# A hybrid decoder layer on one core: the first window group's keys projected transposed, three groups of transfers issued from other places

## The reference

```
u = rmsnorm(x, g_pre) @ w_in                          # (tokens, 10256)
for g, (win, dil) in enumerate(((128, 1), (512, 4), (2048, 16))):
    q, k, v = dq[:, :, g], dk[:, :, g], dv[:, :, g]   # 4 heads of 128
    # prompt: query t reads keys t - dil*m, m = 0..128; the last win rows of (k, v) are an output
    # samples: 8 new queries read keys of a cache of win rows and the new keys
    o_g = softmax(q k^T / sqrt(128)) v ; lse_g
o_b = sum over g of softmax_g(lse) * o_g
m = sigmoid(ga) * (z_a @ w_gla_branch) + sigmoid(gb) * (z_b @ w_dil_branch)
h = x + rmsnorm(m @ w_out, g_post)
y = h + (pe @ w_ple_proj) * sigmoid(h @ w_ple_gate)
```

## Time and profile before

| what | value |
|---|---|
| median of three runs | 2817.8 us (2817.68 to 2823.16) |
| profiled execution, its own time | 2818.61 us |
| its span | 2816.8 us |
| PE busy | 2778.1 us (99%) |
| DVE / ACT / POOL busy | 1080.3 / 871.9 / 386.1 us |
| transfers | 558.36 MB, mean 198 GB/s |

### The profile page before, as it was taken

How to read it: one execution, slowest core, us unless ns; L and a number is a source line. 1 busy time by engine, 2 the same in 40 slices (tenths; PEclk the granted TensorE clock), 3 DMA queues, 4 the chain that set the end, 5 groups by cost and what they waited for, 6 DMA issues and landing times.

```text
span 2816.8 us, 40869 instructions
## 1 busy us (share of the span) xinstructions
PE 2778.1 (99%) x16168; PEld 1458.2 (52%) x16168; DVE 1080.3 (38%) x2401; ACT 871.9 (31%) x1788; POOL 386.1 (14%) x633
## 2 busy tenths in 40 slices
PE   8999999999999999999999989999999899999998
PEld 4444456555545665666555545555544344444444
DVE  6311134444333443344223323333323455555452
ACT  5211034444312222333123321111113444444341
POOL 2000010111311002120011113232200000000000
PEclk9999999999999999999999999999999999999999
DMA  9543454655677566584576759787736966556642
GB/s 282 132 169 130 149 202 151 215 189 202 202 250 275 178 193 205 188 276 157 179 266 219 242 174 326 238 261 244 235 136 199 308 170 174 142 159 178 163 113 57
DMA packets 320399, 558.36 MB, mean 198 GB/s; under 512 B 179114, under 2 KB 184305, under 8 KB 316242
## 3 DMA queue, kind: packets, MB, share of 16 engines
q1 hardware_dynamic: 269154, 296.86, 35.1%
q0 software_dynamic: 51056, 258.89, 27.5%
HBM read 378.96 MB, written 236.79 MB: 219 GB/s over the span
## 4 chain that ended last, share of the span: by engine, by line
PE 95%; DMA 2%; SPq 2%; DVE 1%; issue 0%; POOL 0%; ACT 0%; POOLq 0%; DVEq 0%
PE out L2614 42%; PE out L2183 22%; PE out L2611 15%; PE out L1120 2%; PE out L1105 2%; PE out L2617 2%; PE out L1111 1%; PE out L614 1%; PE out L625 1%; PE out L624 1%; PE out L1403 1%; PE out L1096 1%; PE out L1363 1%; DMA U<-stage 1%; SPq L355 1%; DMA sw_kc<-in_cache_kv_w 0%
## 5 line engine op out<-in xcount | busy, mean ns | idle before, releaser
L2614 PE MATMUL out<-w_hi,xn_hi 128*128 128x512 f16 x1920 | 729.0, 380 | 1.3 <-DVE w_lo L2483 0.7
L2614 PE MATMUL out<-w_lo,xn_hi 128*128 128x512 f16 x1920 | 728.3, 379 | 0.0
L2614 PE MATMUL out<-w_hi,xn_lo 128*128 128x512 f16 x1920 | 728.2, 379 | 0.0
L2514 ACT ACTIVATE stage<-out 128x512 f32<-128x512 f32 (+1 forms) x170 | 99.3, 584 | 900.0 <-PE out L2614 605.4
L2552 DVE TENSOR_SCALAR stage<-out 128x512 f32<-128x512 f32 (+1 forms) x170 | 114.8, 676 | 646.9 <-PE out L2614 424.1
L2614 PEld LDWEIGHTS out<-w_hi,xn_lo 128*128 128x128 f16 x1920 | 188.0, 98 | 227.0 <-issue 0.8
L2614 PEld LDWEIGHTS out<-w_hi,xn_hi 128*128 128x128 f16 x1920 | 188.4, 98 | 207.7 <-issue 6.5
L2614 PEld LDWEIGHTS out<-w_lo,xn_hi 128*128 128x128 f16 x1920 | 188.1, 98 | 200.8 <-issue 0.5
L2611 PE MATMUL out<-xn_hi,w_hi 128*128 128x512 f16 x640 | 242.8, 379 | 0.0
L2611 PE MATMUL out<-xn_hi,w_lo 128*128 128x512 f16 x640 | 242.6, 379 | 0.0
L2611 PE MATMUL out<-xn_lo,w_hi 128*128 128x512 f16 x640 | 242.6, 379 | 0.0
(11 more groups left out here) (318 smaller groups left out, 4007.5 us busy)
## 6 DMA issues: line engine op xcount, KB each, us to landing
out<-in_cache_kv_w POOLq DMA_DIRECT2D x64, 1020.0 KB, 9.6
U<-stage SPq DMA_DIRECT2D x240, 256.0 KB, 4.7
raw<-in_w_in SPq DMA_DIRECT2D x78, 512.0 KB, 5.0
sw_kc<-in_cache_kv_w POOLq DMA_DIRECT2D x24, 1024.0 KB, 12.0
sw_vc<-in_cache_kv_w POOLq DMA_DIRECT2D x24, 1024.0 KB, 9.9
UT<-stage SPq DMA_DIRECT2D x80, 256.0 KB, 3.7
sw_rows<-U POOLq DMA_DIRECT2D x32, 512.0 KB, 7.2
out<-in_cache_kv_w POOLq DMA_DIRECT2D x16, 1008.0 KB, 7.6
```

The costliest lines, as they stand in the source:

```text
L2514: move_out(act, m, lambda o, x: act.activation(o, x, ACT.Copy, scale=1.0 / W_SCALE))
L2614: last = pe.matmul(out[m % 3][:, :], x[:, k, at:at + P], y[:, k, :], start=first, stop=final)
```

## The change

- `U_DK`, the keys of group 0, joins `TURNED`: the 16 prompt tiles of this column come out with features in rows and go to `UT`. For group 0 `load` takes a head's keys from there with one transfer, and the score matmul reads them directly. PE transposes only the last block of each head (four in all), ACT copies it to `kT`, and POOL stores these 128 tokens x 4 heads to the output at step 67 of group 0; ACT waits for that store (`kept_stored`) before it uses `kT` in group 1. POOL's copy of these rows from `U` goes. `load` waits for the scores of the head before last ahead of the keys' load, for all groups.
- The buffers of windows and samples are placed in another order, so that the samples' first loads touch only the buffers of even heads. POOL issues them at slot 515 instead of 522, after `head_done` for head 2 of group 2 and `cutter.done`; the mask's load comes at slot 527, after `windows.done`. DVE begins the samples' buffers after `windows.read`, without waiting for the stores.
- `turn_m(0)` stands in slot 674 right behind `turn_z(1)`, ahead of `turn_pe(1)` and `load_early(2)`, instead of in slot 675.
- `queue_weights` is issued by ACT instead of SP, in the same last slot, also after the projection's last matmul.

```
-TURNED = [U_GQ, U_GK] + [U_DQ + g * WIDTH for g in range(GROUPS)]
+TURNED = [U_GQ, U_GK] + [U_DQ + g * WIDTH for g in range(GROUPS)] + [U_DK]
+T_DK = T_DQ + GROUPS * WIDTH
...
 class Windows:
+    def turns(self, n):
+
+        return n // BLOCKS if n < self.STEPS else HEADS + n - self.STEPS
...
     def load(self, q, g, h):
         s, n = h % 2, g * HEADS + h
-        wait(q, self.turned, (n - 1) * BLOCKS)
-        at = U_DK + g * WIDTH + h * HD
-        for src, dst in self.pieces(self.U[0:SEQ, at:at + HD], self.k[s][:, :, :], g):
-            q.dma_start(dst, src).then_inc(self.k_loaded[s], 16)
+        wait(q, self.turned, self.turns(max((n - 1) * BLOCKS, 0)))
         wait(q, self.scored, (n - 1) * BLOCKS)
+        if g == 0:
+            at = T_DK + h * HD
+            q.dma_start(self.k[s][:, :, :], self.UT[at:at + HD, :].rearrange("p (b i) -> p b i", i=P)).then_inc(self.k_loaded[s], 16)
+        else:
...
+        if g == 0 and r == self.STEPS + 3:
+            q.wait_ge(self.turned_kept, HEADS)
+            q.dma_start(self.kv_prompt[0, 0, :, 0], self.kT[:, :HEADS, :]).then_inc(self.kept_stored, 16)
...
+    def head_done(self, eng, g, h):
+
+        eng.wait_ge(self.summed, (g * HEADS + h + 1) * BLOCKS)
+        eng.wait_ge(self.stored[h % 2], self.moved(g, h))
...
-            wait(pe, self.turned_kept, n)
-            pe.transpose(self.TURN[:, 0:P], self.k[h % 2][:, b, :], self.identity[:, :]).then_inc(self.turned, 1)
+            if g > 0 or b == BLOCKS - 1:
+                wait(pe, self.turned_kept, self.turns(n))
+                pe.transpose(self.TURN[:, 0:P], self.k[h % 2][:, b, :], self.identity[:, :]).then_inc(self.turned, 1)
...
-            pe.wait_ge(self.turned_kept, n + 1)
+            if g > 0:
+                pe.wait_ge(self.turned_kept, self.turns(n + 1))
...
+            kT = self.kT if g > 0 else self.k[h % 2]
...
     def scalar(self, act, g, r):
+            if n == self.STEPS:
+                act.wait_ge(self.kept_stored, 16)
...
+            elif b == BLOCKS - 1:
+                act.wait_ge(self.turned, self.turns(n + 1))
+                act.activation(self.kT[:, h, :], self.TURN[:, 0:P], ACT.Copy).then_inc(self.turned_kept, 1)
...
 class Samples:
     def queue(self, q, r):
-        if r == -5:
+        if r == -12:
             self.load_q(q, 0)
             for p in range(last + 1):
                 self.load_k(q, 0, p)
                 if p == 0:
-                    for x in range(self.RING):
+                    for x in range(3):
                         self.load_rows(q, x)
+        if r == 0:
             q.dma_start(self.mask[:, :], self.mask_in).then_inc(self.mask_loaded, 16)
...
 class Mix:
         if slot == self.MERGE_SLOT + 1:
             self.turn_z(sp, 1)
+            self.turn_m(sp, 0)
             self.turn_pe(sp, 1)
             self.load_early(sp, 2)
...
         if slot == self.MERGE_SLOT + 2:
-            self.turn_m(sp, 0)
...
-            if slot == SAMPLE_SLOT - 5:
+            if slot == SAMPLE_SLOT - 12:
+                windows.head_done(q, GROUPS - 1, HEADS - 2)
+                cutter.done(q)
+            if slot == SAMPLE_SLOT:
                 windows.done(q)
-                cutter.done(q)
...
         def _(sp):
-                if m == COLUMN_TILES * TOKEN_TILES - 1 and half == 1:
-                    for i in range(2):
-                        sp.wait_ge(out_ready[i], COLUMN_TILES * TOKEN_TILES // 2)
-                    mix.queue_weights(sp)
...
         def _(act):
+                    if half == 1 and m == COLUMN_TILES * TOKEN_TILES - 1:
+                        for i in range(2):
+                            act.wait_ge(out_ready[i], COLUMN_TILES * TOKEN_TILES // 2)
+                        mix.queue_weights(act)
```

More of the change, by code:

```diff
@@ L1013, in __init__ @@
         self.result_kept = one("result_kept")
+        self.kept_stored = one("kept_stored")
+    def turns(self, n):
+        return n // BLOCKS if n < self.STEPS else HEADS + n - self.STEPS
     def moves(self, g):
@@ L1075, in left, with read @@
         n = GROUPS * self.STEPS
-        return [(signal, n) for signal in (self.turned, self.turned_kept, self.scored, self.masked, self.top_ready, self.weighed,
+        return [(self.turned, self.turns(n)), (self.turned_kept, self.turns(n))] + [(signal, n) for signal in (self.scored, self.masked, self.top_ready, self.weighed,
                                            self.prob_turned, self.prob_kept, self.summed, self.result_kept)]
+    def head_done(self, eng, g, h):
+        eng.wait_ge(self.summed, (g * HEADS + h + 1) * BLOCKS)
+        eng.wait_ge(self.stored[h % 2], self.moved(g, h))
+    def read(self, eng):
+        eng.wait_ge(self.summed, GROUPS * self.STEPS)
+        eng.wait_ge(self.result_kept, GROUPS * self.STEPS)
     def done(self, eng):
-        wait(eng, self.summed, GROUPS * self.STEPS)
-        for h in range(HEADS - 2, HEADS):
-            wait(eng, self.stored[h % 2], self.moved(GROUPS - 1, h))
+        self.head_done(eng, GROUPS - 1, HEADS - 2)
+        self.head_done(eng, GROUPS - 1, HEADS - 1)
     def at(self, g, i):
@@ L1126, in scalar @@
             n, h, b, _, dil = self.at(g, r)
-            act.wait_ge(self.turned, n + 1)
-            wait(act, self.scored, n - 1)
-            if dil > 1:
+            if n == self.STEPS:
+                act.wait_ge(self.kept_stored, 16)
+            if g > 0:
+                act.wait_ge(self.turned, self.turns(n + 1))
+                wait(act, self.scored, n - 1)
                 if b == 0:
@@ L1192, in __init__ @@
         self.q_places = [(tile, QUAD) for tile in (self.new_k, self.new_v, sb("sw_q", [P, WIDTH]))]
+        self.rows = [sb(f"sw_rows{s}", [P, self.PAIR, WIDTH]) for s in range(self.RING)]
+        self.vc = sb("sw_vc", [P, N_CACHE, WIDTH])
         self.qT = sb("sw_qT", [P, GROUPS * HEADS, QUAD])
         self.kT = [sb(f"sw_kT{s}", [P, HEADS, P]) for s in range(2)]
-        self.rows = [sb(f"sw_rows{s}", [P, self.PAIR, WIDTH]) for s in range(self.RING)]
         self.sT = [sb(f"sw_sT{i}", [P, P]) for i in range(len(ROWED))]
@@ L2263, in run_layer @@
             with ExitStack() as part:
[L2264 removed]
+                windows = Windows((core.bind(part)[0], sem), side, U, UT, a["window_mask"], identity, OG, kv_prompt[0])
         stores = Stores(sem)
@@ L2467, in _ @@
                 mix.pool(pool, t)
-            pool.wait_ge(copied, SHIFTS + 4 * GROUPS * 16)
+            pool.wait_ge(copied, SHIFTS + (4 * GROUPS - 1) * 16)
         def cut_hi_piece(act, i):
@@ L2581, in _ @@
                 if q == SAMPLE_SLOT - 2:
-                    windows.done(dve)
+                    windows.read(dve)
                     samples.start(dve)
```

23 lines of the change are left out of this document (12 added, 11 removed).

## The result

The changed kernel takes 2803.8 us (median of 5 runs, 2802.1 to 2805.0), the kernel before on the same chip 2818.5 (5 runs, 2817.7 to 2823.2): the ratio is 0.9946, interval [0.9935, 0.9958]. It is faster by 14.6 us, where I had forecast 24. The profiled execution took 2802.4 us (before 2818.6), with a span of 2800.5 (before 2816.8).

A forecast was written before the change was run, and what follows sets the result against it. PE, 99% busy, was taken as the bound: its instructions plus three waits. Savings of 6.4 + 10.1 + 7.1 = 23.6 us took the profiled 2818.6 to 2795.0, the median to 2794 us; range 2788 to 2802.

The forecast's parts named there:

- Part 1: Group 0's keys projected transposed: 60 of 64 transpositions on PE go, 0.107 us each, saving 6.4 us.
- rival C: Group 1: ACT's wait for the kept keys' store holds up PE and makes the kernel slower; chance 0.02.
- rival D: Group 0: the keys' transpositions were free, so their removal gives 0 and the time is 2800.6 us; chance 0.05.
- Part 2: Samples' first loads issued earlier by POOL: PE's 8.1 us wait and 2.0 us of half speed go, 10.1 us.
- Part 3: After the last slot: weights on ACT and m of tile 0 turned earlier start branches(2) sooner, saving 7.1 us.
- rival B: After the last slot: weights starve tile 2's loads, PE starts as before, gain there 0, time 2801.3 us; chance 0.11.

The follow-up runs named there:

- m_only: Changed kernel with the weights issued by SP again, m of tile 0 still turned ahead of tile 2's loads; 2800.5 us, ratio 0.9935.
- w_only: Changed kernel with m of tile 0 turned in slot 675 again, behind tile 2's loads, weights still on ACT; 2801.6 us, ratio 0.9939.
- rows_8k: Changed kernel with each weight transfer on ACT cut in two of 1 MB, rows of 8 KB instead of 16 KB; 2802.6 us, one run.
- ahead: Changed kernel with tile 2's loads and the transpositions of z(1) and pe(1) issued by SP two slots sooner; 2799.8 us, ratio 0.9932.
- ahead_z: Kernel of ahead with z(2)'s transposition also put before SP's wait for the last tile's store; 2791.2 us, ratio 0.9900.
- p1_only: Changed kernel with only the transposed keys of group 0 kept; samples' loads, m and weights issued as before; 2809.7 us, ratio 0.9967.
- p3_undone: Changed kernel with m of tile 0 turned in slot 675 and the weights issued by SP again; 2800.2 us, ratio 0.9934.
- early_first: Changed kernel with tile 2's five loads issued ahead of the three turns on SP; 2800.1 us, ratio 0.9931.
- rows_2k: Changed kernel with each weight transfer on ACT cut in eight of 256 KB, rows of 2 KB instead of 16 KB; 2801.6 us, ratio 0.9939.

## Why the prediction was wrong

- **Part 1** was right: 6.4 forecast, 6.3 measured in three kernels, from group 0's first score matmul to the samples' first. ACT's new wait shows nowhere (rival C), the transpositions were not free (rival D).
- **Part 2** was right in mechanism and size: 10.1 forecast, 10.2 measured from the samples' first matmul to T. The wait is gone, and so is the half speed behind it: the granted clock stays at 1.00 from 1668 to 1680, and the 12 matmuls behind the first cached keys go from 1675.86 to 1678.45, in 2.6 us, where they took 4.1 before.
- **Part 3** was wrong: 7.1 forecast, 0.2 measured. The first step that failed is "Loads (2.2 MB) and an equal share of weights at 422 GB/s take 10.4 us instead of 5.2; a part of that is hidden by the time to issue, and I take 2.7 of the 5.2." From T + 3.8 to T + 19.6 are 15.8 us. By 3.7 of them m's turn moved the loads' issue (T - 5.8 to T - 2.1; I had 6.2), and 12.1 are the sharing, which m_only and w_only show only where both edits meet. The share was not equal but went by packets, 75% to the weights; SP's later loads took little of the rest (its queue moved 2.46 MB from T - 2.2 to T + 19.5, tile 2's loads have 2.24). So z of tile 2 was ready at T + 31.1, not T + 24.3.
- From there to PE's start I had 7.1 us, and it was 5.7; the half speed behind it, 1.5 us, I had not counted.
- The second step that failed is "With the weights elsewhere that store is through before 2194.5", that is T + 24.3. No sum stood behind it. In the changed kernel the store holds SP until T + 28.9, in two pieces with a median of 23.9 us to land, where I had expected well under 18.59. It cost nothing there, since z was later still. But by itself it would have taken much of the forecast gain: rows_8k has z ready at T + 25.1, near my T + 24.3, and branches(2) at T + 37.1. Once z is early, it costs 8.6 us (ahead against ahead_z). My own bytes said as much: 6.3 MB of weights and some 4 MB of SP's at 422 GB/s give an estimate of T + 24.4 for the last of them, no sooner.
- The weights I had right in kind: 3.7 us of wait forecast, 2.1 measured.

What happened is rival B, to which I gave 0.11 with 2801.3 us. It had z ready at 2201.7 counted in before's time, and T + 31.1 is 2201.3 there; its sign, a wait for z of 8 us or more, is there with 8.6; my range ended at 2802, and the profiled execution took 2802.4. Against B I had written that the store held up for 18.6 us "was order within a queue, not between two". That was the error of reading: one row showed an order within a queue, and I took it as a reason that two queues share fairly, for which no row spoke. (The rule of the Trainium skill that I weighed, "DMA: Bandwidth & Descriptors", section "Issuing engines are not separate DMA queues", that issuing from several engines only saves the issuing time, held for the bandwidth: 430 GB/s in one stretch with both queues against 446 and 422 with one in the earlier trace rows. It says nothing of who gets it.) The last 1.4 us to the median of 2803.8 lie between executions of one kernel.

Open: p1_only and p3_undone run before's order behind T, and are still 2.1 to 2.5 us shorter there (644.5 and 644.1 against 646.6). In before the weights leave SP 1.1 us later and the second half of m's turn takes 6.50 us to issue instead of 3.97 and 4.28; I have one trace of before, so it can be the execution or the kernel. The times lean to the kernel: p3_undone's median lies 19.3 us below before's on the same chip, and only 15.9 of these lie ahead of T. If so, part 3 costs these 2 us, and parts 1 and 2 bring them in a way that no run here explains.

## What to carry to other kernels

Moving a large transfer to another engine's queue takes it out of the order, not out of the way: before the move, look what else the first queue has in flight at that moment, and issue what is wanted soon so early that it has landed, transposing DMAs and small stores above all. Between two busy queues estimate shares from the length of the packets, not from equal parts. Where an engine waits for a store before its next issue, and the other queue is full, put what doesn't need the store ahead of the wait.

## What the runs showed of the hardware that I had not expected

- Two queues at a DMA share near 1: for each packet of q1 q10 had 0.56 to 0.62 of its own, with rows of 16, 8 and 2 KB, so 75, 62 and 27% of the bytes. In other stretches the number lay between 0.41 and 1.07.
- The last tile's store, pieces of 64 KB, took 23.9 us to land beside 6 MB on the other queue (the changed kernel), and 18.6 behind the same 6 MB on its own queue (before).
- A transposing DMA suffers beside long rows on the other queue. In w_only its issue alone held SP for 11.10 and 12.70 us, instead of 1.65 and 1.34 in the changed kernel; in early_first its landing took 20.7 instead of 3.3, at packets of some 230 bytes.
- Issuing 24 transfers of 256 KB held ACT for 20 us, 0.8 us each, where three of 2 MB took 1.4 us (rows_2k, and the changed kernel).
